# Expert pairs side by side, four experts gathered transposed, whole rows scattered, low residual halves in place

## The chip, the core and the metric

One NeuronCore of a Trainium2 chip runs the kernel. It has TensorE (matmuls, written to the eight banks of PSUM), VectorE, ScalarE, GpSimd, SyncE (here only issuing transfers) and 16 DMA engines. The metric is the time of one launch on the device in microseconds, the median of several runs; lower is better. All data are float32.
## The reference

A decoder layer on 512 tokens of width 1024: a mixing block (RG-LRU and pooling branches), then a mixture of experts, then a gated input embedding and a last norm. What matters here is the middle:

```python
u = rms_norm(h, norm_ffn_g[l])
# hierarchical_moe: best group of 4, best 2 of its 8 experts, for each token
expert_ids = g_idx[:, None] * EXPERTS_PER_GROUP + top_i      # 512 tokens x 2 choices, 32 experts
...
def expert_block(args):
    xblk, e = args
    h = jax.nn.silu(xblk @ w_gate_e[e]) * (xblk @ w_up_e[e])  # 1024 -> 512, twice
    return h @ w_down_e[e]                                    # 512 -> 1024
contrib = y[dest] * w_s[:, None]
return jax.ops.segment_sum(contrib, tok_s, num_segments=n)
...
h = h + moe_out
u = rms_norm(h, norm_ple_g[l])
h = h + sigmoid(u @ w_ple_gate[l]) * (p[l] @ w_ple[l])
```

## The kernel before

The program is one straight order of instructions for each engine, with semaphores between them. The first 355 us compute the mixing block. Matmuls there are made exact by splitting each operand in a high half and a low residual half (`split_high` on ScalarE, `split_low`), three fp32r products per matrix. The last two of its 15 weight blocks ("out") give the residual stream h1, whose rows are split too: `row_high` and `rows_split` (L364) write `rows_high` and `rows_low`. `transpose_h1` (L1256) and `logits` (L1268) make the router's logits, `route` the choices, `places` (L1279) and `find_places` the place of each token among the (at most 64 per round, C = 64) tokens of its expert.

Then comes a loop over the 32 experts, in rounds of 64 tokens for each; one round does in this case. All tokens sit in SBUF, and each expert's are picked by a matmul with a 0/1 matrix `pick` that VectorE makes (`make_pick`, L1017) for two experts at a time. `gather` multiplies `rows_high` and `rows_low` with it (stationary: pick, 128 columns for two experts; moving: 512 columns of the rows). ScalarE copies the gathered rows with their norm's scale (`gather_scale`, `copy_rows`, L764), TensorE transposes them (`transpose_x`, L1363), VectorE writes `xT` with the norm's gain (`copy_xT`, L1028). `gate_and_up` (L1375) multiplies one expert's 64 tokens with its gate and up matrices; the 64 tokens fill half of the array's columns, so two column halves of the weights run side by side. ScalarE takes the sigmoid, VectorE the two products, TensorE transposes the hidden rows (`transpose_hidden`, L1404), and `down` (L1390) of the expert before runs in between. VectorE scales the result by the gate (`scale_y`, L1108), and GpSimd scatters it to memory by row number, as half rows of 2 KB (`y_halves`), 128 of them for each expert. The row numbers and gates are gathered like the rows (`gather_info`).

Every matrix of an expert is a transfer of 2 MB (96 in all), issued by SyncE in the order in which TensorE wants them (`loads`) into a ring of nine slots (`LEAD`), `expert_slots`. Load n waits until load n - 9 has been read: a semaphore that TensorE raises after gate, up or down of that expert. The first loads wait for the end of the blocks before, the eighth and ninth for the logits and for the last `rows_split`, since their slots hold h1T and h1.

After the loop: the scatter's end, eight loads of the scattered rows, h1 restored from its halves, `add_choice` (L1159) for the sums, norm and transposes, and eight groups of 24 matmuls with the gate matrix `w_ple_gate`, which is split in high and low too (`gate_high`, `gate_low`, L357, in four steps).

All matmuls go through one helper, so they all stand at L1210 of the profile and are told apart by their tiles: `ring,junk` is gate or up, `ring,hT` down, `rounded,pick` the gather, `rstd,pick` the scale, `info,pick` row and gate, L1366 and L1407 the transposes of gathered and hidden rows. A name is the operand that moves first, then the stationary one.

## Time and profile before

| | us |
|---|---|
| median of 3 runs (lowest, highest) | 932.99 (931.66, 933.77) |
| the profiled execution's own time | 931.2 |
| its span, first to last instruction | 929.5 |
| TensorE busy, of the span | 896.1 (96%) |
| VectorE, ScalarE, GpSimd busy | 381.6, 243.5, 102.9 |
| DMA, mean over the span | 274 GB/s |
| granted clock of TensorE, mean | 0.991 |

All that follows comes from one profiled execution. Its times are microseconds from the first instruction, and differences between the execution's own time and the median belong to the run, not to the kernel. A busy TensorE is not one at its peak: matmuls overlap, and the time between the starts of two is what one costs.

### The profile page before, as it was taken

The numbers are of one execution on the slowest core, as the hardware profiler recorded it, in microseconds if no ns is written. First come the engines' busy times: TensorE is split into PE (matmuls) and PEld (weight loads), VectorE is DVE, ScalarE is ACT, GpSimd is POOL, SyncE is SP. The second block draws the span as 40 slices with busy tenths as digits, with TensorE's granted clock in tenths as the row PEclk, the third lists the DMA queues.
The fourth block names the chain that finished last, engine by engine and source line by source line (L and its number), as shares of the span: only waits on it lengthen the run. The fifth ranks groups of instructions, "written<-read, shape, count | busy, mean of one in ns | idle before, by whom it ended". The sixth has DMA issues, their size and how long they took to land.

```text
span 929.5 us, 12845 instructions
## 1 busy us (share of the span) xinstructions
PE 896.1 (96%) x5471; PEld 604.6 (65%) x5471; DVE 381.6 (41%) x617; ACT 243.5 (26%) x334; POOL 102.9 (11%) x80
## 2 busy tenths in 40 slices
PE   4999899999999997999999999999999999999996
PEld 3778677787888886656555555556555555554575
DVE  6699429953643427122212222122212222123875
ACT  6565337633332233100000000000000000001557
POOL 3338560000000000000000000000000000001000
PEclk9999999999999998999999999999999999999999
DMA  9222222212424446999999999999999999981702
GB/s 257 88 84 91 90 91 91 90 46 81 146 91 181 181 181 274 430 426 426 426 427 427 428 425 426 427 430 425 427 426 427 426 429 428 425 354 44 294 1 91
DMA packets 43297, 254.54 MB, mean 274 GB/s; under 512 B 8722, under 2 KB 9814, under 8 KB 30952
## 3 DMA queue, kind: packets, MB, share of 16 engines
q1 hardware_dynamic: 40392, 248.47, 65.7%
q0 software_dynamic: 2560, 4.20, 1.2%
q10 hardware_dynamic: 288, 1.05, 0.3%
q8 instruction: 43, 0.70, 0.3%
q14 instruction: 14, 0.11, 0.0%
HBM read 247.41 MB, written 10.49 MB: 277 GB/s over the span
## 4 chain that ended last, share of the span: by engine, by line
PE 86%; DVE 8%; ACT 3%; DMA 2%; issue 1%; DVEq 0%; SPq 0%; POOLq 0%; ACTq 0%
PE bank L1210 81%; PE bank L1366 2%; DVE ring L916 1%; PE bank L1407 1%; DVE ring L920 1%; DVE r L922 1%; ACT ring_rounded L345 1%; DVE ring_rounded L350 1%; DMA r<-in_x_dram 1%; DMA ring<-in_w_up_b_dram 1%; PE bank L1223 1%; DMA ring<-expert_rows 0%; DVE r L854 0%; PE bank L1264 0%; DVE ring L921 0%
## 5 line engine op out<-in xcount | busy, mean ns | idle before, releaser
L1210 PE MATMUL bank<-ring_rounded,ring_rounded 128*128 128x512 f32 x768 | 251.0, 392 | 1.7 <-ACT r L796 1.7
L1210 PE MATMUL bank<-r_rounded,ring_rounded 128*128 128x512 f32 x704 | 231.3, 399 | 4.7 <-DVE ring_rounded L350 2.8
L1210 PEld LDWEIGHTS bank<-ring_rounded,ring_rounded 128*128 128x128 f32 x768 | 144.6, 189 | 34.3 <-issue 2.4
L1210 PE MATMUL bank<-ring,junk 128*64 128x256 f32 x1408 | 166.1, 389 | 0.4 <-DVE junk L1030 0.4
L1210 PEld LDWEIGHTS bank<-r_rounded,ring_rounded 128*128 128x128 f32 x704 | 133.3, 190 | 36.5 <-DVE ring_rounded L350 3.6
L1210 PEld LDWEIGHTS bank<-ring,junk 128*64 128x64 f32 x1408 | 96.6, 134 | 61.4 <-issue 3.5
L1210 PE MATMUL bank<-ring,hT 128*64 128x512 f32 x512 | 119.8, 599 | 0.9 <-DVE hT L1115 0.9
L781 ACT ACTIVATE sig<-bank 128x256 f32<-128x256 f32 x32 | 12.3, 384 | 369.0 <-PE bank L1210 369.0
L591 POOL DMA_INDIRECT expert_rows<-r,row_i x32 | 31.7, 990 | 690.0 <-DVE r L1111 690.0
L1126 DVE TENSOR_TENSOR sig<-sig,bank 128x256 f32<-128x256 f32 x32 | 13.5, 421 | 218.3 <-ACT sig L781 218.3
L1210 PE MATMUL bank<-r,junk 128*64 128x256 f32 x640 | 76.4, 389 | 0.0
L350 DVE TENSOR_TENSOR ring_rounded<-ring,ring_rounded 128x2048 fp32r<-128x2048 f32 x19 | 43.5, 2288 | 55.1 <-ACT ring_rounded L345 55.1
L345 ACT ACTIVATE ring_rounded<-ring 128x2048 fp32r<-128x2048 f32 x28 | 53.6, 1913 | 43.8 <-DMA ring<-in_w_in_dram 19.2
L1210 PEld LDWEIGHTS bank<-ring,hT 128*64 128x64 f32 x512 | 32.9, 137 | 48.5 <-issue 46.6
L1210 PEld LDWEIGHTS bank<-r,junk 128*64 128x64 f32 x640 | 43.5, 134 | 28.1 <-issue 1.7
L1210 PE MATMUL bank<-r_rounded,pick 128*128 128x512 f32 x136 | 57.6, 425 | 0.0
L1210 PE MATMUL bank<-ring_rounded,pick 128*128 128x512 f32 x136 | 54.3, 401 | 0.0
L1111 DVE TENSOR_SCALAR r<-bank,gate_c 128x512 f32<-128x512 f32 x32 | 24.0, 751 | 70.3 <-PE bank L1210 70.3
L350 POOL TENSOR_TENSOR ring_rounded<-ring,ring_rounded 128x2048 fp32r<-128x2048 f32 x9 | 42.4, 4730 | 62.4 <-ACT ring_rounded L345 62.4
L1030 DVE TENSOR_TENSOR junk<-bank,gain_col 128x512 f32<-128x512 f32 x34 | 23.4, 691 | 52.6 <-PE bank L1366 52.6
L767 ACT ACTIVATE gain<-bank,row_scale 128x512 f32<-128x512 f32 x34 | 23.3, 687 | 73.4 <-PE bank L1210 73.4
L1210 PEld LDWEIGHTS bank<-r_rounded,pick 128*128 128x128 f32 x136 | 26.1, 192 | 11.2 <-issue 6.5
(195 smaller groups left out, 780.9 us busy)
## 6 DMA issues: line engine op xcount, KB each, us to landing
ring<-in_w_down_e_dram SPq DMA_DIRECT2D x32, 2048.0 KB, 14.5
ring<-in_w_gate_e_dram SPq DMA_DIRECT2D x22, 2048.0 KB, 11.8
ring<-in_w_up_e_dram SPq DMA_DIRECT2D x22, 2048.0 KB, 16.8
r<-in_w_up_e_dram SPq DMA_DIRECT2D x10, 2048.0 KB, 17.8
r<-in_w_gate_e_dram SPq DMA_DIRECT2D x10, 2048.0 KB
ring<-in_w_in_dram SPq DMA_DIRECT2D x18, 1024.0 KB, 7.3
r<-in_x_dram SPq DMA_DIRECT2D x8, 512.0 KB, 8.0
ring<-in_w_up_a_dram SPq DMA_DIRECT2D x4, 1024.0 KB, 6.3
```

What stands on the lines that cost most here:

```text
L345: nc.scalar.activation(high_half(n, h), whole_half(n, h), ACT.Copy).then_inc(high_ready, 1)
L350: api.tensor_tensor(low_half(n, h), whole_half(n, h), high_half(n, h), ALU.subtract).then_inc(low_ready[low_engine[n, h]], 1)
L591: nc.gpsimd.indirect_dma_start(out=y_halves, out_offset=bass.IndirectOffsetOnAxis(ap=row_i[:, e:e + 1], axis=0), in_=yrow[:, e % 4, :], in ...
L767: nc.scalar.activation(xrow[:, h * HALF:(h + 1) * HALF], bank[6 + h][:, :], ACT.Copy, scale=row_scale[:, 0:1]).then_inc(xrow_ready, 1)
L781: nc.scalar.activation(sig[:, :], bank[2 + e % 2][:, 0:FE // 2], ACT.Sigmoid).then_inc(sig_ready, 1)
L916: after(v.reciprocal(q, q))
L920: after(v.tensor_tensor(t, t, q, ALU.mult))
L1030: v.tensor_tensor(xT[:, 4 * h:4 * h + 4, :, :].rearrange("p k e c -> p k (e c)"), bank[6 + h][:, :].rearrange("p (k n) -> p k n", k=4), bc ...
L1111: v.tensor_scalar(yrow[:, e % 4, :], bank[5][:, :], gate_c[:, e:e + 1], None, ALU.mult).then_inc(y_stored, 1)
L1126: v.tensor_tensor(sig[:, :], sig[:, :], gate_up[:, 0:FE // 2], ALU.mult).then_inc(gated, 1)
L1210: return nc.tensor.matmul(*a, **k)
L1366: ins = nc.tensor.transpose(bank[6 + h][:, k * P:(k + 1) * P], xrow[:, h * HALF:(h + 1) * HALF].rearrange("p (q j) -> p j q", j=4)[:, k, : ...
```

## The change

- Experts run in pairs: `gate_or_up` and `down` stream the matrices of two experts side by side, 512 columns each, instead of two halves of one. The load order is changed to match, and a slot is given back when both experts of the pair have been read.
- Four experts (a "team") are gathered at once, and directly transposed: the rows are the stationary operand (one word of eight, `gather_k`), the pick matrix of 256 columns moves. Scale gather, row copy and `transpose_x` go; ScalarE copies PSUM to `xT` with the gain, and the scale of the norm is applied behind the gate and up products (`factor`). The first gather waits for all low halves before its second part.
- The scatter takes whole rows of 4 KB, both experts of a pair at once, 16 times instead of 32; two row buffers instead of four.
- `rows_low` is written in place of h1, and h1T moves to a smaller buffer, so that slots 1 and 2 of the ring (tiles 6 and 7) are free when the last two blocks start. The first load is issued one block sooner, two more by the next, and none waits for logits or residuals.
- The last two down matrices are loaded in halves. The gate matrix of the last stage gets its low half in place; all four steps of it are loaded ahead of the scattered rows and split before the first sum.

```diff
-    loads = [(0, 0), (1, 0)]
-    for e in range(1, NE):
-        loads += [(0, e), (1, e), (2, e - 1)]
-    loads += [(2, NE - 1)]
+    loads = [(which, e) for which in range(2) for e in range(2)]
+    for first in range(2, NE, 2):
+        loads += [(which, e) for which in range(2) for e in (first, first + 1)] + [(2, first - 2), (2, first - 1)]
+    loads += [(2, NE - 2), (2, NE - 1)]
     load_of = {matrix: n for n, matrix in enumerate(loads)}
...
-        yrow = r4[:, 0:4 * HALF].rearrange("p (b d) -> p b d", b=4)
-        xT = junk[:, :].rearrange("p (k e c) -> p k e c", k=KD, e=2)
-        xrow = gain[:, :]
+        yrow = r4[:, 0:2 * D].rearrange("p (b d) -> p b d", b=2)
+        def xT(k):
+            return (gain, junk)[k // 4][:, k % 4 * TEAM * C:(k % 4 + 1) * TEAM * C]
         rows_high = r2_r[:, :].rearrange("p (i d) -> p i d", i=TT)
-        rows_low = slot_r[6][:, :].rearrange("p (i d) -> p i d", i=TT)
-        pick = sb("pick", [P, 2, TT, 2, C], F32R)
-        hT = sb("hT", [P, KF, C])
-        sig = sb("sig", [P, FE // 2])
-        hid = sb("hid", [P, FE // 2])
+        rows_low = r1_r[:, :].rearrange("p (i d) -> p i d", i=TT)
+        pick = sb("pick", [P, TT, TEAM, C], F32R)
+        hT = sb("hT", [P, KF, 2 * C])
+        sig = sb("sig", [P, FE])
...
-        expert_slots = [ring[:, 0, :], ring[:, 3, :], ring[:, 4, :], ring[:, 1, :], ring[:, 2, :], ring[:, 5, :], r3[:, :],
-                        ring[:, 7, :], r1[:, :]]
+        expert_slots = [ring[:, 0, :], ring[:, 6, :], ring[:, 7, :], ring[:, 3, :], ring[:, 4, :], ring[:, 1, :], ring[:, 2, :],
+                        ring[:, 5, :], r3[:, :]]
...
             dve.wait_ge(rows_high_ready, i + 1)
+            dve.wait_ge(rows_psum, 2 * i + 2)
             nc.vector.tensor_tensor(rows_low[:, i, :], h1[:, i, :], rows_high[:, i, :], ALU.subtract).then_inc(rows_low_ready, 1)
...
+                    load_expert(0)
+            for n in range(1, LEAD):
+                sp.wait_ge(tile_done, 4 * (FIRST_OUT if n < 3 else FIRST_OUT + 1 if n < 5 else len(blocks)))
                 load_expert(n)
...
+                    sp.wait_ge((gate_psum, gate_up_psum, y_psum)[which], n0 + (e // 2 + 1))
+                for n in range(LEAD, 3 * NE - 2):
                     wait_expert_read(n - LEAD)
                     load_expert(n)
+                for n in (3 * NE - 2, 3 * NE - 1):
+                    wait_expert_read(n - LEAD)
+                    load_last_half(n, 0)
+                for n in (3 * NE - 2, 3 * NE - 1):
+                    load_last_half(n, 1)
...
-                    wait_expert_read(max(range(7, 3 * NE, LEAD)))
+                    wait_expert_read(max(range(6, 3 * NE, LEAD)))
                     sp.dma_start(wple, w_ple[0].rearrange("(k p) n -> p k n", p=P)).then_inc(ple_in, 16)
                     sp.dma_start(p_rows, p[0, 0].rearrange("(i p) n -> p i n", p=P)).then_inc(ple_in, 16)
-                    wait_expert_read(max(range(0, 3 * NE, LEAD)))
-                    load_gate(0)
-                    load_gate(1)
-            sp.wait_ge(row_free, rounds * NE + 4)
+                    wait_expert_read(max(range(8, 3 * NE, LEAD)))
+                    for step in range(4):
+                        load_gate(step)
+            sp.wait_ge(row_free, rounds * PAIRS + 2)
             for i in range(TT):
                 for k in range(2):
                     sp.dma_start(y_back(i, k), y_rows[k * S + i * P:k * S + (i + 1) * P, :]).then_inc(y_in[k][i], 16)
...
-                    pool.wait_ge(y_stored, n0 + (e + 2))
+                n0 = pool.snap(r * PAIRS)
+                for m in range(PAIRS):
+                    pool.wait_ge(y_stored, n0 * 2 + (2 * m + 4))
                     pool.sem_inc(rows_taken, 1)
                     nc.gpsimd.indirect_dma_start(
-                        out=y_halves, out_offset=bass.IndirectOffsetOnAxis(ap=row_i[:, e:e + 1], axis=0),
-                        in_=yrow[:, e % 4, :], in_offset=None, bounds_check=last_row,
-                        oob_is_err=False).then_inc(scattered[e % 4], 16)
-                    if e >= 2:
-                        release_row(n0, e - 2)
-                for e in (NE - 2, NE - 1):
-                    release_row(n0, e)
+                        out=y_rows, out_offset=bass.IndirectOffsetOnAxis(ap=row_i[:, m:m + 1], axis=0),
+                        in_=yrow[:, m % 2, :], in_offset=None, bounds_check=last_row,
...
+            def copy_xT(at, k, bank_):
+                act.wait_ge(xT_psum, at + (k // 2 + 1))
+                nc.scalar.activation(xT(k), bank_[:, k % 2 * TEAM * C:(k % 2 + 1) * TEAM * C], ACT.Copy,
+                                     scale=gain_col[:, k:k + 1]).then_inc(xT_ready, 1)
+            def sigmoid(n0, m):
+                act.wait_ge(factor_ready, n0 + (m + 1))
+                act.wait_ge(gate_psum, n0 + (m + 1))
+                if m >= 1:
+                    act.wait_ge(hT_psum, n0 + m)
+                nc.scalar.activation(sig[:, :], bank[2][:, :], ACT.Sigmoid, scale=factor[:, m, 1:2]).then_inc(sig_ready, 1)
+            for k in range(KD):
+                copy_xT(0, k, bank[4 + k // 2])
...
-            gate_high(0)
-            gate_high(1)
+            for step in range(4):
+                gate_high(step)
...
-                if i >= 2:
-                    gate_high(i)
...
-            def make_pick(pair, at=slice(0, TT)):
+            def make_pick(team, at=slice(0, TT)):
 
                 n = at.stop - at.start
-                v.tensor_tensor(pick[:, pair % 2, at, :, :], iota[:, :].unsqueeze(1).unsqueeze(1).to_broadcast([P, n, 2, C]),
-                                where.unsqueeze(3).to_broadcast([P, n, 2, C]), ALU.is_equal).then_inc(pick_ready, 1)
+                where = place[:, TEAM * team:TEAM * (team + 1), at].rearrange("p e i -> p i e")
+                v.tensor_tensor(pick[:, at, :, :], iota[:, :].unsqueeze(1).unsqueeze(1).to_broadcast([P, n, TEAM, C]),
+                                where.unsqueeze(3).to_broadcast([P, n, TEAM, C]), ALU.is_equal).then_inc(pick_ready, 1)
...
+            def take_info(n0, m):
+                dve.wait_ge(info_psum, n0 + (m // 2 * 2 + 2))
+                got = bank[5][:, m % 2 * 4:m % 2 * 4 + 3]
+                v.tensor_copy(factor[:, m, :], got[:, 1:3]).then_inc(factor_ready, 1)
+                v.tensor_scalar(row_i[:, m:m + 1], got[:, 0:1], row_base[:, 0:1], None, ALU.add).then_inc(row_ready, 1)
+            def make_hidden(n0, m):
+                dve.wait_ge(sig_ready, n0 + (m + 1))
+                v.scalar_tensor_tensor(out=sig[:, :], in0=bank[2][:, :], scalar=factor[:, m, 1:2], in1=sig[:, :], op0=ALU.mult,
+                                       op1=ALU.mult).then_inc(gated, 1)
+                dve.wait_ge(gated, n0 + (m + 1))
+                dve.wait_ge(gate_up_psum, n0 + (m + 1))
+                v.scalar_tensor_tensor(out=sig[:, :], in0=bank[3][:, :], scalar=factor[:, m, 1:2], in1=sig[:, :], op0=ALU.mult,
+                                       op1=ALU.mult).then_inc(hidden_ready, 1)
+            def scale_y(n0, m):
+                dve.wait_ge(y_psum, n0 + (m + 1))
+                dve.wait_ge(row_free, n0 + (m + 1))
+                for h in range(2):
+                    v.tensor_scalar(yrow[:, m % 2, h * HALF:(h + 1) * HALF], bank[h][:, :], factor[:, m, 0:1], None,
+                                    ALU.mult).then_inc(y_stored, 1)
+            def copy_hT(n0, m):
+                dve.wait_ge(hT_psum, n0 + (m + 1))
+                v.tensor_copy(hT[:, :, :], bank[4][:, :].rearrange("p (k c) -> p k c", k=KF)).then_inc(hT_ready, 1)
...
+                n0 = dve.snap(r * PAIRS)
+                for team in range(TEAMS):
+                    take_info(n0, 2 * team)
+                    take_info(n0, 2 * team + 1)
+                    make_pick((team + 1) % TEAMS)
+                    for m in (2 * team, 2 * team + 1):
+                        make_hidden(n0, m)
+                        if m >= 1:
+                            scale_y(n0, m - 1)
+                        copy_hT(n0, m)
+                scale_y(n0, PAIRS - 1)
...
-            gate_low(dve, v, 0)
-            gate_low(dve, v, 1)
+            for step in range(4):
+                gate_low(dve, v, step)
...
-                if i >= 2:
-                    gate_low(dve, v, i)
...
+            def gather_k(dst, k, i, **flags):
+                for part in (rows_high, rows_low):
+                    ins = mm(dst[:, k % 2 * TEAM * C:(k % 2 + 1) * TEAM * C],
+                             part[:, i, :].rearrange("p (q k) -> p k q", k=KD)[:, k, :],
+                             pick[:, i, :, :].rearrange("p e c -> p (e c)"), start=flags["start"] and part is rows_high,
+                             stop=flags["stop"] and part is rows_low)
+                return ins
+            def gather(at):
+                for k in range(KD):
+                    if k >= 4 and k % 2 == 0:
+                        pe.wait_ge(xT_ready, at + (k - 2))
+                    for i in range(TT):
+                        ins = gather_k(bank[6 + k // 2 % 2], k, i, start=(i == 0), stop=(i == TT - 1))
+                    if k % 2 == 1:
+                        ins.then_inc(xT_psum, 1)
...
+                    for e in (2 * m, 2 * m + 1):
+                        ins = mm(bank[5][e % 2 * C:(e % 2 + 1) * C, m % 2 * 4:m % 2 * 4 + 3], pick[:, i, e % TEAM, :].bitcast(F32),
+                                 info[:, e, i, :], start=(i == 0), stop=(i == TT - 1))
...
+            def gate_or_up(r, n0, m, which):
+                experts = (2 * m, 2 * m + 1)
+                for e in experts:
+                    wait_landed(r, load_of[which, e])
+                if which == 0 and m >= 1:
+                    pe.wait_ge(hidden_ready, n0 + m)
+                for k in range(KD):
+                    if which == 0 and m % 2 == 0:
+                        pe.wait_ge(xT_ready, n0 * 4 + (4 * m + k + 1))
+                    for e in experts:
+                        w = wslot(load_of[which, e], KD)
+                        ins = mm(bank[2 + which][e % 2 * C:(e % 2 + 1) * C, :], xT(k)[:, e % TEAM * C:(e % TEAM + 1) * C], w[:, k, :],
+                                 start=(k == 0), stop=(k == KD - 1))
+                ins.then_inc(gate_up_psum if which else gate_psum, 1)
+            def down(r, n0, m):
+                experts = (2 * m, 2 * m + 1)
+                pe.wait_ge(y_stored, n0 * 2 + (2 * m + 2))
+                pe.wait_ge(hT_ready, n0 + (m + 1))
+                if m == PAIRS - 1:
+                    pe.wait_ge(last_half, r * 32 + 32)
+                for k in range(KF):
+                    if k == (KF // 2 if m == PAIRS - 1 else 0):
+                        for e in experts:
+                            wait_landed(r, load_of[2, e])
                     for h in range(2):
-                        ins = mm(bank[5][h * C:(h + 1) * C, :], hT[:, k, :], w[:, k, h * HALF:(h + 1) * HALF],
-                                 start=(k == 0), stop=(k == KF - 1))
-                if ks[-1] == KF - 1:
-                    ins.then_inc(y_psum, 1)
-            def transpose_hidden(n0, e):
-                pe.wait_ge(hidden_ready, n0 + (e + 1))
-                for j in range(2):
-                    ins = nc.tensor.transpose(bank[4][:, j * P:(j + 1) * P], hid[:, j * P:(j + 1) * P], ident[:, :])
+                        for e in experts:
+                            ins = mm(bank[h][e % 2 * C:(e % 2 + 1) * C, :], hT[:, k, e % 2 * C:(e % 2 + 1) * C],
+                                     wslot(load_of[2, e], KF)[:, k, h * HALF:(h + 1) * HALF], start=(k == 0), stop=(k == KF - 1))
+                ins.then_inc(y_psum, 1)
+            def transpose_hidden(n0, m):
+                pe.wait_ge(hidden_ready, n0 + (m + 1))
+                if m >= 1:
+                    pe.wait_ge(hT_ready, n0 + m)
+                for k in range(KF):
+                    ins = nc.tensor.transpose(bank[4][:, k * P:(k + 1) * P], sig[:, :].rearrange("p (q k) -> p k q", k=KF)[:, k, :],
+                                              ident[:, :])
...
-            for h in range(2):
+            for k in range(KD):
                 for i in range(2):
-                    gather_from(0, h, i, rows_high, start=(i == 0), stop=False)
-                    gather_from(0, h, i, rows_low, start=False, stop=False)
+                    gather_k(bank[4 + k // 2], k, i, start=(i == 0 and k % 2 == 0), stop=False)
             places(1)
             pe.wait_ge(pick_ready, 2)
+            for k in range(KD):
+                for i in range(2, TT):
+                    ins = gather_k(bank[4 + k // 2], k, i, start=False, stop=(i == TT - 1 and k % 2 == 1))
+                if k % 2 == 1:
+                    ins.then_inc(xT_psum, 1)
...
+                n0 = pe.snap(r * PAIRS)
+                for team in range(TEAMS):
+                    gate_or_up(r, n0, 2 * team, 0)
+                    if team == 0:
+                        pe.wait_ge(info_made, 3)
+                    else:
+                        pe.wait_ge(row_ready, n0 + 2 * team)
+                    gather_info(2 * team)
+                    gather_info(2 * team + 1)
+                    gate_or_up(r, n0, 2 * team, 1)
+                    if team >= 1:
+                        down(r, n0, 2 * team - 1)
+                    transpose_hidden(n0, 2 * team)
+                    for which in range(2):
+                        gate_or_up(r, n0, 2 * team + 1, which)
+                    pe.wait_ge(pick_ready, r * TEAMS + (team + 3))
+                    gather(n0 * 4 + KD * (team + 1))
+                    down(r, n0, 2 * team)
+                    transpose_hidden(n0, 2 * team + 1)
+                down(r, n0, PAIRS - 1)
```

## Rows read from the trace of the kernel before

**Rows 1.** Windows, 461 to 551 us: each engine's busy time, clock, DMA share, GB/s.
```profile
461.00:551.00 90.00, 90.00 (x688) 51.32 (x686) 20.20 (x49) 6.43 (x12) 5.86 (x6) 1.00 1.01 427
```

**Rows 2.** Waits of SyncE's DMA queue, 365 to 860: us, times, longest.
```profile
SPq L456 <- PE bank L1210: 406.5, 87, 8.2
```

**Rows 3.** Timeline of SyncE: start, us, issue of a down matrix.
```profile
355.62 0.43 SPq L456 DMA_DIRECT2D ring<-in_w_down_e_dram  x1
...
805.20 4.47 SPq L456 DMA_DIRECT2D ring<-in_w_down_e_dram  x2
```

**Rows 4.** DMA issues of those moments: size, us from issue to landing.
```profile
ring<-in_w_down_e_dram SPq DMA_DIRECT2D x1, 2048.0 KB, 12.9
...
ring<-in_w_down_e_dram SPq DMA_DIRECT2D x1, 2048.0 KB, 18.6
```

**Rows 5.** Timeline of TensorE and VectorE, 581 to 596: start, busy us.
```profile
581.88 0.68 DVE L1021 TENSOR_TENSOR pick<-iota,place 128x512 fp32r<-128x512 f32 x1
...
588.53 1.05 PE L1210 MATMUL bank<-rstd,pick 128*128 128x1 f32 x8
...
589.45 0.48 PE L1210 MATMUL bank<-r_rounded,pick 128*128 128x512 f32 x1
...
589.76 0.39 PE L1210 MATMUL bank<-ring_rounded,pick 128*128 128x512 f32 x1
...
591.15 0.39 PE L1210 MATMUL bank<-ring_rounded,pick 128*128 128x512 f32 x1
...
591.47 0.63 PE L1210 MATMUL bank<-info,pick 128*64 128x2 f32 x16
...
591.96 3.63 PE L1210 MATMUL bank<-ring,hT 128*64 128x512 f32 x16
...
595.52 0.44 PE L1407 MATMUL bank<-ident,hid 128*128 128x128 f32 x2
```

**Rows 6.** Timeline of TensorE, 335 to 341: transposes of h1 and logits.
```profile
335.04 1.04 PE L1264 MATMUL bank<-ident,r 128*128 128x128 f32 x8
...
335.83 0.48 PE L1210 MATMUL bank<-ring_rounded,ring_rounded 128*128 128x512 f32 x1
...
338.67 1.87 PE L1210 MATMUL bank<-wrt,ring 128*128 128x36 f32 x16
...
340.37 0.48 PE L1210 MATMUL bank<-ring_rounded,ring_rounded 128*128 128x512 f32 x1
```

**Rows 7.** Timeline of TensorE and VectorE, the start of the loop.
```profile
362.20 0.40 PE L1210 MATMUL bank<-ring_rounded,pick 128*128 128x512 f32 x1
...
367.40 1.87 PE L1210 MATMUL bank<-rstd,pick 128*128 128x1 f32 x8 [1.03 <-DVE pick L1021]
...
375.05 1.12 PE L1210 MATMUL bank<-ring,junk 128*64 128x256 f32 x8 [0.42 <-DVE junk L1030]
...
366.92 0.42 DVE L1021 TENSOR_TENSOR pick<-iota,place 128x256 fp32r<-128x256 f32 x1
367.26 1.22 DVE L367 TENSOR_TENSOR ring_rounded<-r,r_rounded 128x1024 fp32r<-128x1024 f32 x1
```

**Rows 8.** Windows of 1 us, the start of the loop; clock third from last.
```profile
367.00:368.00 1.00, 0.60 (x3) 0.60 (x4) 1.00 (x2) 0.00 (x0) 0.00 (x0) 0.50 0.88 377
...
373.00:374.00 1.00, 0.70 (x5) 0.70 (x6) 0.00 (x0) 0.98 (x3) 0.00 (x0) 0.73 1.03 442
```

**Rows 9.** Timeline, 851 to 872: last down, low halves, first sums.
```profile
851.55 3.65 PE L1210 MATMUL bank<-ring,hT 128*64 128x512 f32 x16 [0.91 <-DVE hT L1115]
...
861.41 4.49 DVE L361 TENSOR_TENSOR ring_rounded<-ring,ring_rounded 128x2048 fp32r<-128x2048 f32 x2
...
865.82 3.62 DVE L1159 TENSOR_TENSOR r<-r,ring 128x1024 f32<-128x1024 f32 x3
...
871.54 1.06 PE L1223 MATMUL bank<-ident,r 128*128 128x128 f32 x8 [0.46 <-DVE r L854]
```

**Rows 10.** Window of 2 us in the last stage.
```profile
890.00:892.00 2.00, 1.18 (x10) 1.04 (x10) 0.91 (x1) 0.34 (x1) 0.00 (x0) 1.00 0.00 0
```

281 lines of the change are left out of this document (71 added, 210 removed).

## The prediction, on record before the changed kernel was seen

> **What bounds the kernel now.** I read four views in order. The windows come first: from 461 to 551 us TensorE is busy 90.00 of 90 us at full clock, and in the same window the DMA engines have a share of 1.01 at 427 GB/s [rows 1]. Two resources are full at once, so the question is which of them sets the end. The waits of the DMA queue answer half of it: SyncE, which issues the expert loads, waited 87 times and 406.5 us for TensorE to give a slot back [rows 2]. So TensorE paces the loop. The issue times and landings give the other half. Load 4 is issued at 355.62 and lands 12.9 us later, at 368.5. Load 94 is issued at 805.20 and lands 18.6 us later, at 823.8 [rows 3, 4]. That is 90 loads in 455.3 us, 5.06 us a load of 2.1 MB, and the time from issue to landing has grown: the transfers are slightly slower than TensorE and eat the ring's lead, without making it wait. A load alone cannot take under 2.1 MB / 427 GB/s = 4.91 us [rows 1]. The loop runs from 375.05 to 851.55 + 3.65 = 855.2 us [rows 7, 9], 30.0 us for two experts; the transfers want 6 x 5.06 = 30.4. Making TensorE faster therefore hands the loop to the DMA engines almost at once, and the loop's end then follows from when the loads start and how fast they run. The tail after 855.2 is 74.3 us of a span of 929.5.
>
> **TensorE's work for four experts, after.** Now: 2 x 30.0 = 60.0 us for four. After the change:
> - Gate, up and down are the same streams, 512 columns wide, two experts side by side. One down now is 16 instructions from 591.96 to 595.52, 3.56 us [rows 5]; a matrix of a pair is 32 of those, 7.12 less one handover of some 0.1: 7.05. Gate and up have the same count of columns as two downs each. Six pairs of matrices: 42.3 us.
> - The scale gather goes: 588.53 to the first gather at 589.45, 0.9 us a pair [rows 5], 1.8 for four. The transposes of the gathered rows go: 8 per pair in two groups. Eight transposes of h1 take 335.83 - 335.04 = 0.79 us [rows 6]; with 0.2 us of handover each group of four is 0.6, 2.4 for the four groups.
> - Gathers of row and gate: 0.49 each [rows 5], four now, two after: 0.98.
> - Transposes of the hidden rows: two groups of four at 0.6 and a little: 1.3, against four groups of two at 0.44 [rows 5].
> - The gather itself is what no row shows. Now it is 32 matmuls for four experts, 128 stationary columns and 512 moving: (591.15 - 589.76) / 6 = 0.232 us each [rows 5], 7.4 us. After it is 64 with 256 moving columns: the same columns, twice the weight loads. From below: half of 0.232 is 0.116, and matmuls of 36 columns with 128-wide stationary operands still take (340.37 - 338.67) / 16 = 0.106 us [rows 6], which is the weight load's own pace. From above: 0.232, as if nothing were won by the shorter stream. I take 0.13, the longer of stream (256 columns at 2.4 GHz, 0.107) and load (0.106) plus the 0.02 that the 512-column matmul has over its own 512 / 2.4 GHz = 0.213: 8.3 us. It is near the low end because loads are hidden in the 512-column rows: 0.106 of load and 0.213 of stream add to 0.32 there, and 0.232 is measured.
> - Sum: 42.3 + 8.3 + 1.0 + 1.3 = 52.9 us against 60.0.
>
> The Trainium skill speaks against this change at the gather. "TensorE: Matmul & The Clock Gate", Part 3, says that a weight load overlaps a running matmul only when the two use different row groups; these all use the full array. By that rule each gather matmul would cost load plus stream, 0.214 us, and 13.7 us for four experts. The 512-column rows already disagree with it (0.232, not 0.32), but no row shows a stream as short as its load, so the rule stays a rival. "SBUF — State Buffer", on 16-byte cachelines, says that reads which step past a line each time pay a penalty, and the new stationary operand takes every eighth word. The trace disagrees at this speed: the transposes of h1 have just such a stationary operand, one word of eight, and go at 0.79 / 8 = 0.099 us each [rows 6], no slower than the dense ones of the logits. I add nothing for it.
>
> **The transfers, after.** Twelve loads per four experts: 60.7 us against TensorE's 52.9, so the DMA engines bind. Loads 0 to 4 are now in before 355 us (three before), and loads 5 to 8 go at 355.3: four x 4.91 + 0.9 of latency end at 376. Load 9 needs the slot of expert 0's gate matrix, and that comes free, together with that of expert 1, only when the first pair's gate is done. The DMA engines idle until then; the head start of two loads is spent here.
>
> When is that? The second half of the first gather waits for the last low residual, now before its first matmul. VectorE's chain is 0.26 us longer by the selection, twice as wide (256 columns take 0.42 [rows 7], 512 take 0.68 [rows 5]), so the residual of 1.22 us that started at 367.26 [rows 7] ends at 368.8. TensorE's clock is then at half (0.50 at 367, 0.73 at 373 [rows 8]), so 32 matmuls x 0.213 = 6.8 us: gate starts at 375.6, against 375.05 [rows 7], because the scaled rows and their transposes are no longer behind the gather. The first half of the gather (32 x 0.13 = 4.2 us) lies in the wait before the second routing half. If the load does not hide at half clock this is 13.7 and the start 382.5.
>
> Gate of pair 0 ends at 375.6 + 7.05 = 382.7, load 9 starts. Loads 9 to 91 (up of the last pair) are 83 x 5.06 = 420.0 us, plus 0.9 latency and 2.5 by which a load in a queue lands after its turn (load 4 landed at 368.5; two loads from 355.25 are 355.25 + 0.9 + 9.8 = 366.0). That is 806.1. The nine slots suffice: the longest stretch with none given back is gather plus down, 8.3 + 7.05 = 15.4 us, three loads' worth. TensorE, with 7.8 us to spare per four experts, has caught up with the transfers after about three teams and then waits 2 to 3 us at a time. After load 91: up 7.05, the round's last gather (which nobody needs) 8.3, down 7.05, last down 7.05 = 29.5. Between the two downs VectorE must evict two banks (2 x 0.75) and copy the transposed hidden rows (0.7), and the last down waits for that copy: 2.3. The last loads land by 825 and bind nothing. End of the loop 806.1 + 31.8 = 837.9 instead of 855.2: **-17.3 us**.
>
> **The tail gives some back.** Before the first sum of expert rows (865.82) VectorE stood at the two low halves of the last gate matrix, 861.41 + 4.49 = 865.9 [rows 9]: it was exactly busy until the rows came. After, all four low halves lie ahead of the sums (+4.49), and the last expert rows take two evictions instead of one (+0.75, with the scatter behind them): +5.2 us. TensorE, done with the input embedding, waited 0.46 us there for the transposes at 871.54 [rows 9]; after, this idle becomes 5.7 us. The idle from 362.6 to 367.4 (with the few small matmuls of the routing in it) was some 4.8 us and left the clock at half until 373.7 [rows 7, 8], so I add half of the first 3.5 us of the last stage, 1.7. Back comes the wait at 890 to 892 (1.18 of 2.00 us busy [rows 10]), in which a low half stood in the way: -0.8. Tail: +5.2 + 1.7 - 0.8 = **+6.1**.
>
> Costed at nothing: whole rows in the scatter (same bytes, half the issues), GpSimd's work, ScalarE's eight copies per team (under the gather and the down behind it), the extra copy into the routing info (under the first gather). If the scatter's share of the DMA time (5.06 - 4.91 = 0.15 us a load) vanished, the loop would end 12 us sooner; half of it is all I allow.
>
> **Sum.** -17.3 + 6.1 = -11.2 us. The profiled execution took 931.2 us by its own time, span 929.5; this gives 920.0. The median shown is 932.99, 1.8 above it, so the forecast is **922 us**. A difference of under 0.2% (1.9 us) can't be told from none.
>
> **Rivals.**
> 1. Transfers bind, and they are quicker than now because whole rows scatter more cheaply, or the tail keeps its clock: 6 us of the scatter's 12 and the 1.7 of the clock: 914. For it: fewer, larger pieces; against it: the bytes are the same.
> 2. The weight load of the gather is not hidden (0.214 us). TensorE takes 44.6 + 13.7 = 58.3 us a team, 466 for eight; start at 382.5; with the 1.7 between the last downs the loop ends at 851. With the tail of 74.3 + 6.1 that is a span of 931, in the terms of the median **935**: no change. This is the page's rule above. Against it the 512-column rows; for it that nothing shorter has been seen.
> 3. Slower: a gather matmul costs what one of 512 columns costs, 0.232 or more, because the pace is that of the strided stationary read. Team 44.6 + 14.8 = 59.4, eight 475, start 383 (32 x 0.46 at half clock, from 368.8), loop end 860; with the tail **944**. It decides from a pitch of 0.21 up with that start (383 + 8 x (44.6 + 64 p) + 1.7 + 6.1 = 855.2), of 0.225 with the start at 375.6.
> 4. Each wait for a load drops the clock. A wait of 3 us is shorter than the idle that did it; and a slow team eats its own slack of 7.8 us, after which there is no wait. Only the last 30 us lie open: +3, 925. Inside the range of the forecast.
>
> **Numbers.** Forecast with rival 4: 0.62 (own range 916 to 930). Rival 1: 0.10. Rival 2: 0.14, spread from 929 to 938. Rival 3: 0.14. Faster by over 0.2%: 0.62 + 0.10 + a third of rival 2 = 0.77. Within 0.2%: 0.06, out of rival 2 (931 to 935). Slower: 0.17, rival 3 and the rest of rival 2. The range 913 to 937 leaves out rival 3 and a little at each end.
>
> **What would show it.** The gather: 64 starts per team, 0.13 us apart. SyncE's waits for TensorE shrink and TensorE shows idle time before gate, up and down, released by a DMA, from about 540 us on. The windows stay at 427 GB/s until about 825 us, with one dip at 376 to 383. The loop ends near 838. In the tail four low halves stand in a row before the first sum, and TensorE idles some 5 us before the first transposes. Wrong would make it: a pitch over 0.2; a start later than 377; a DMA rate under 427 in the loop; slots that starve the transfers.

## The result, and the profile after

The changed kernel takes **941.98 us** (median of 4 runs, 940.96 to 942.31) against 933.0 us (4 runs beside it, 931.66 to 933.77): ratio 1.0096, 95% interval 1.0078 to 1.0113. It is slower by 1%. The forecast was 922 in a range of 913 to 937, with 0.77 on faster; the price of rival 3, 944, is 2 us off. The profiled execution has a span of 940.6 us (929.5 before).

The first place to look is the one that no row of before could show: a team's gather. From the timeline of TensorE, changed kernel (start, busy us; a matmul's own bar is longer than the distance to the next):

```profile
410.04 15.68 PE L1209 MATMUL bank<-pick,r_rounded 128*128 128x256 f32 x64
425.65 0.64 PE L1209 MATMUL bank<-r,hT 128*64 128x512 f32 x1
```

64 gather matmuls in 425.65 - 410.04 = 15.61 us are **0.244 us each**, not 0.13: dearer than the 0.232 of a matmul with twice the columns [rows 5]. The chain of work that ended last shows the teams, one after another (start, us, what):

```profile
432.74 0.68 PE bank L1401 x4
433.42 21.68 PE bank L1209 x127
455.10 0.68 PE bank L1401 x4
455.79 36.57 PE bank L1209 x160
492.35 0.68 PE bank L1401 x4
```

It has matmuls and transposes alone. A team is 492.35 - 432.74 = 59.6 us; of that 15.6 is gather and 44.0 the rest, which the prediction had at 44.6. The windows and the waits of SyncE's queue, from 365 to 860 us, say the same from their side (columns as in [rows 1] and [rows 2]):

```profile
373.00:461.00 88.00, 87.06 (x451) 45.41 (x452) 13.46 (x28) 10.07 (x20) 2.15 (x2) 0.97 0.82 339
461.00:551.00 90.00, 90.00 (x432) 51.42 (x430) 10.04 (x17) 8.79 (x19) 1.93 (x2) 1.00 1.00 424
```

```profile
SPq L427 <- PE bank L1209: 394.6, 43, 21.9
```

TensorE is busy 90.00 of 90 us as before [rows 1], and the queue still waits for it, now in fewer and longer waits (43 and 394.6 us; 87 and 406.5 before [rows 2]). From 461 on the two kernels look alike; a lower rate stands earlier, 339 GB/s from 373 to 461 (427 in that stretch before). It comes from the start of the loop (timeline of TensorE, then of SyncE's queue):

```profile
361.05 7.92 PE L1209 MATMUL bank<-pick,r_rounded 128*128 128x256 f32 x32
368.82 0.19 PE L1209 MATMUL bank<-routed_bf,before 128*128 128x32 bf16 x1
...
371.79 7.94 PE L1209 MATMUL bank<-pick,r_rounded 128*128 128x256 f32 x32 [2.53 <-DVE r_rounded L373]
379.66 2.79 PE L1209 MATMUL bank<-ring,gain 128*64 128x512 f32 x12
```

```profile
356.90 0.62 SPq L427 DMA_DIRECT2D r<-in_w_down_e_dram  x1
386.79 0.33 SPq L427 DMA_DIRECT2D ring<-in_w_down_e_dram  x1
```

The first half gather takes 7.8 us, so the place sums wait for it and start only at 368.82; the second half takes 379.66 - 371.79 = 7.87 more. Gate starts at 379.66 (375.05 before [rows 7], forecast 375.6), load 9 goes at 386.79 (forecast 382.7). The windows of 2 us hold one more fact:

```profile
365.00:367.00 2.00, 2.00 (x10) 1.00 1.00 422
...
374.00:376.00 2.00, 2.00 (x10) 0.50 0.99 426
...
420.00:422.00 2.00, 2.00 (x10) 1.00 1.00 426
```

With 256 columns a stream would need at least 0.107 us at 2.4 GHz and 0.213 at 1.2, but the gather keeps its pace at a granted clock of 0.50 and of 1.00: 10 matmuls are to be seen in 2 us in each (all that have a part in the window, so more than start in it). The second half gather took 7.87 us with some 5.8 of them at 0.50, the first 7.8 with some 3 at 0.50, and a team's 15.6 are at 1.00 throughout. So neither a stream nor a sum of load and stream in TensorE's clock sets the pace; what does is for the experiments.

The last down (timeline of TensorE):

```profile
852.33 7.09 PE L1209 MATMUL bank<-ring,hT 128*64 128x512 f32 x32 [1.61 <-DVE hT L1127]
```

It ends at 859.4 (855.2 before), +4.2. From gate's start to there it is 479.8 us, against 480.2 before: the loop itself gains 0.4 us, and its start is 4.6 later. Then the tail (timeline of VectorE, then of TensorE; answers to [rows 9]):

```profile
865.92 4.49 DVE L366 TENSOR_TENSOR ring_rounded<-ring,ring_rounded 128x2048 fp32r<-128x2048 f32 x2
870.32 4.49 DVE L366 TENSOR_TENSOR r_rounded<-r,ring_rounded 128x2048 fp32r<-128x2048 f32 x2
874.72 2.48 DVE L1160 TENSOR_TENSOR r<-r,ring 128x1024 f32<-128x1024 f32 x2
```

```profile
880.45 1.94 PE L1222 MATMUL bank<-ident,r 128*128 128x128 f32 x8 [4.87 <-DVE r L866]
884.05 5.49 PE L1209 MATMUL bank<-ring_rounded,ring_rounded 128*128 128x512 f32 x12 [1.66 <-ACT ring L810]
```

The four low halves stand in a row before the first sum, TensorE waits 4.87 us (forecast 5.7, before 0.46), and comes back at half clock: 12 matmuls in 5.49 us. Tail: 940.6 - 859.4 = 81.2, against 74.3: +6.9 (forecast +6.1). The +4.2 at the loop's end and the tail's +6.9 are the 11.1 us between the two spans.

### The profile page after: what moved, and what is told of

Same layout as the page of the kernel before. It is cut to its first block, busy times and chain, and to the rows that moved or that the text cites. A ratio compares the mean times of both kernels' runs of the same rounds, so it can differ in the third digit from the quotient of the medians.

```text
span 940.6 us, 10137 instructions
## 1 busy us (share of the span) xinstructions
PE 904.1 (96%) x4223; PEld 592.0 (63%) x4223; DVE 341.2 (36%) x478; ACT 249.3 (27%) x356; POOL 87.5 (9%) x63
## 4 chain that ended last, share of the span: by engine, by line
PE 88%; DVE 8%; ACT 2%; DMA 1%; issue 1%; DVEq 0%; SPq 0%; POOLq 0%; ACTq 0%
PE bank L1209 85%; DVE ring L928 1%; DVE ring L932 1%; PE bank L1401 1%; PE bank L1222 1%; DVE r L934 1%; DMA r<-in_x_dram 1%; DMA ring<-expert_rows 0%; DVE r_rounded L366 0%; DVE ring_rounded L355 0%; PE bank L1263 0%; ACT ring_rounded L350 0%; DMA expert_rows<-r,row_i 0%; DVE ring L933 0%; ACT junk L623 0%
## 5 line engine op out<-in xcount | busy, mean ns | idle before, releaser
L1209 PEld LDWEIGHTS bank<-pick,r_rounded 128*128 128x128 f32 x576 | 139.8, 338 | 9.1 <-issue 9.1
L1209 PE MATMUL bank<-pick,r_rounded 128*128 128x256 f32 x576 | 141.7, 409 | 2.5 <-DVE r_rounded L373 2.5
L1209 PE MATMUL bank<-ring,gain 128*64 128x512 f32 x472 | 116.3, 596 | 0.0
L1209 PE MATMUL bank<-ring,junk 128*64 128x512 f32 x472 | 115.3, 592 | 0.0
L1122 DVE TENSOR_SCALAR r<-bank,factor 128x512 f32<-128x512 f32 x32 | 22.6, 746 | 224.6 <-PE bank L1209 224.6
L600 POOL DMA_INDIRECT expert_rows<-r,row_i x16 | 16.4, 1027 | 710.6 <-DVE r L1122 411.5
L1209 PEld LDWEIGHTS bank<-ring,junk 128*64 128x64 f32 x472 | 36.5, 137 | 73.1 <-issue 73.1
L1209 PEld LDWEIGHTS bank<-ring,gain 128*64 128x64 f32 x472 | 34.4, 137 | 61.3 <-issue 59.4
L1209 PE MATMUL bank<-r,hT 128*64 128x512 f32 x80 | 35.3, 594 | 0.0
L914 DVE SCALAR_TENSOR_TENSOR ring<-bank,prm,ring 128x511 f32<-128x511 f32 (+2 forms) x24 | 17.9, 747 | 36.3 <-ACT ring L659 35.7
```

The lines of the kernel that those rows point to most:

```text
L600: nc.gpsimd.indirect_dma_start(out=y_rows, out_offset=bass.IndirectOffsetOnAxis(ap=row_i[:, m:m + 1], axis=0), in_=yrow[:, m % 2, :], in_o ...
L914: ins = v.scalar_tensor_tensor(out=y[:, d:S], in0=z[:, 0:S - d], scalar=tap(3 - d, c), in1=y[:, d:S], op0=ALU.mult, op1=ALU.add)
L1122: v.tensor_scalar(yrow[:, m % 2, h * HALF:(h + 1) * HALF], bank[h][:, :], factor[:, m, 0:1], None, ALU.mult).then_inc(y_stored, 1)
L1209: return nc.tensor.matmul(*a, **k)
```

## The experiments

Each is compared with the kernel before, run beside it on the same chip (medians 931.9 to 932.5). Edits are to the changed kernel.

**1. A ladder of steps.** The two theories for the 0.244: the step between the words of the stationary operand (32 bytes), or the full-array weight load that isn't hidden behind a short stream (rival 2). The gather reads a step of 1, 2, 4 and 8 words for the four pairs of k (other features than the reference's), and so do the router's logits. One execution, 934.7 us.

```
- part[:, i, :].rearrange("p (q k) -> p k q", k=KD)[:, k, :]
+ part[:, i, 0:P * 2 ** (k // 2)].rearrange("p (q s) -> p s q", s=2 ** (k // 2))[:, 0, :]
```

> What it changes in the computation: in the changed kernel the stationary operand of each gather matmul is read with a step of 1, 2, 4 or 8 words for k = 0-1, 2-3, 4-5, 6-7 (always the same first words), and so is the stationary operand of the router's plain f32 logits, so the gathered and routed values are others. The profile after shows 0.244 us from start to start of the 256-column gather matmuls, at full clock (414.7) and at half clock (374) alike. Theory A (the strided read of the stationary fp32r operand sets the pace, at a clock that TensorE's gate doesn't touch): about 0.13 us at step 1, rising with the step to 0.244 at step 8. Theory B (a short stream can't hide its weight load: load plus stream plus handover, 0.106 + 0.107 + 0.02 to 0.03): 0.23 to 0.25 at every step, step 1 too. Theory C (the fp32r kind of weight load is slow in itself, 0.24, and 512-column streams hid it): the same at every step, like B, but independent of the clock. For the f32 logits, 0.106 us dense: A without a difference of kinds gives 0.2 or more at step 8; if fp32r alone suffers, it stays at 0.10 to 0.11.

The timeline of TensorE and windows of 1 us of its gather matmuls (busy, matmuls of which a part lies in it, clock, DMA share, GB/s), team 1:

```profile
415.14 11.70 PE L1209 MATMUL bank<-pick,r_rounded 128*128 128x256 f32 x64
```

```profile
418.10:419.10 1.00, 1.00 (x11) 1.00 1.00 426
419.10:420.10 1.00, 1.00 (x7) 1.00 1.03 442
420.10:421.10 1.00, 1.00 (x6) 1.00 0.96 410
```

There is one edge, halfway. Windows with the steps of 1 and 2 show 10 or 11 matmuls, those with 4 and 8 show 6, as everywhere in the changed kernel's gathers. 32 x 0.123 + 32 x 0.244 = 11.7 us, the whole bar. A step of 4 words costs what a step of 8 does, a step of 2 costs nothing. The logits' stationary operand is plain float32: 32 of them took 5.52 us where the changed kernel's dense ones take 3.7, so it is no matter of the rounded type. Nor does it need a long stream. The logits move 36 columns; of 16 of them, which took 339.65 to 342.37, the 8 at steps of 4 and 8 words cost (2.72 - 8 x 0.106) / 8 = 0.23 us each, an estimate with the dense ones at their pace of [rows 6].

**2. Dense stationary, and nothing else.** The gathers and no other reader take 128 adjacent words, so experts see features in another order than their weights.

```
+ part[:, i, k * P:(k + 1) * P]
```

> What it changes in the computation: the stationary operand of the gather is 128 neighbouring words of the row instead of every eighth, so the features come out in another order than the weights expect; all else is the changed kernel. Theory A (strided stationary read): gather pitch 0.13 us, TensorE 43.7 + 8.3 = 52 us a team instead of 59.3, the loop becomes bound by the transfers (60.7 us a team from 386 on would end up at 806 + 32 = 838 to 842), loop start 376 instead of 379.7, median 922 to 926. Theories B and C (no dependence on the step): pitch 0.24, median 942 as the changed kernel.

919.38 us (917.7 to 920.7), ratio 0.9866 (0.9847 to 0.9885). Timeline and windows:

```profile
405.11 7.94 PE L1209 MATMUL bank<-pick,r_rounded 128*128 128x256 f32 x64
412.98 0.64 PE L1209 MATMUL bank<-r,hT 128*64 128x512 f32 x1
```

```profile
461.00:551.00 90.00, 85.97 (x497) 38.38 (x495) 15.58 (x28) 7.94 (x17) 3.11 (x4) 1.00 1.01 428
```

64 in 7.87 us, **0.123** each, 0.01 from what was forecast. Rival 2, a load that isn't hidden, is gone with it: a full load of 0.106 [rows 6] and a stream of 0.107 fit into 0.123 only if they overlap. TensorE now stands idle here for 4.0 us of 90, and for 8.9, 9.1 and 10.9 in the next three windows, while the DMA engines stay at 426 to 428 GB/s: the transfers bind, and the last down ends at 835.7 (forecast 837.9). The tail keeps its 80.9. So the rest of the prediction's arithmetic held: it said 922, and the chip with a dense gather says 919.

Some of the waits also drop the clock, which the prediction had not expected of waits of 3 us. One of them (timeline of TensorE, then a window of 2 us with the columns of [rows 1]):

```profile
602.14 8.78 PE L1209 MATMUL bank<-ring,hT 128*64 128x512 f32 x32 [2.39 <-DMA ring<-in_w_down_e_dram]
```

```profile
603.00:605.00 2.00, 2.00 (x6) 0.49 (x4) 0.00 (x0) 0.00 (x0) 0.00 (x0) 0.50 0.95 397
```

The down takes 8.78 us, not 7.09. Behind a wait of 3.56 us at 622.68 the clock is at half again; behind one of 2.30 at 562.28 it stayed at 1.00, and what decides it no run here shows. The last down comes no later for it than forecast: TensorE has this time to spare behind the transfers.

**3. Dense by another layout of the weights.** The whole computation, with partition q of a gate or up tile holding rows k times 128 plus q; the gathers and the transposes of h1 read dense, and the 16 KB pieces of the gate and up loads become 2 KB. The down loads, a third of the bytes, keep theirs.

```
- w[0, e].rearrange("(p k) n -> p (k n)", p=P)
+ w[0, e].rearrange("(k p) n -> p k n", p=P)
```

> The same dense stationary operand with the features kept right: gate, up, router weights and the norm's gain are laid out with feature k*128+p at partition p, so gate and up arrive in pieces of 2 KB a row instead of 16 KB in one. The full computation. Theory A: as the dense gather, 922 to 926, if pieces of 2 KB go at the same 427 GB/s. A rival inside it: the smaller pieces cost bandwidth; then SyncE's transfers fall below 420 GB/s in the middle of the loop and the time follows them, 5% less bandwidth being some 16 us on two thirds of the bytes, 935 to 942. Theories B and C: 942.

946.81 us, ratio 1.0166 (1.0147 to 1.0185): slower than either.

```profile
461.00:551.00 90.00, 81.52 (x453) 36.05 (x453) 13.57 (x25) 7.11 (x15) 2.89 (x3) 0.96 1.04 401
```

The gather is at 0.123 and TensorE idle a tenth of the time, but the DMA engines, just as full (1.04), now move 401 GB/s. From gate's start to the end of the last down, at 864.3, the loop takes 6.5% longer than in experiment 2, and the pace of the transfers is 6% lower. The transposes of h1, which now read dense (timeline):

```profile
335.35 1.03 PE L1265 MATMUL bank<-ident,r 128*128 128x128 f32 x8
336.14 0.48 PE L1211 MATMUL bank<-ring_rounded,ring_rounded 128*128 128x512 f32 x1
```

**4. The tail alone.** Gate steps 2 and 3 go back behind the sums of tiles 2 and 3, on ScalarE and VectorE.

```
- for step in range(4):
-     gate_low(dve, v, step)
+ gate_low(dve, v, 0)
+ gate_low(dve, v, 1)
...
+ if i >= 2:
+     gate_low(dve, v, i)
```

> The changed kernel with steps 2 and 3 of the last gate matrix split where the kernel before had them (behind the transposes of row blocks 2 and 3) instead of ahead of the first sum. The tail after the last down is 81.2 us in the changed kernel and 74.3 before. Theory: the two low halves (4.5 us) in front of the first sum, and the half clock that the longer idle causes, are 6 of these 6.9 us: the first sum starts at 870.3 instead of 874.7, no half clock at 881 to 889, median 935.5 to 937.5. Rival: the first sum waits for the scattered rows anyway (they are issued at 865.3, 5.9 us after the last down against 5.05 before) and the gain is under 2 us, 940 or more.

935.9 us (935.2 to 936.8), ratio 1.0044 (1.0027 to 1.006), 6.1 us off the changed kernel. VectorE and TensorE:

```profile
869.92 3.62 DVE L1162 TENSOR_TENSOR r<-r,ring 128x1024 f32<-128x1024 f32 x3
```

```profile
875.64 1.06 PE L1226 MATMUL bank<-ident,r 128*128 128x128 f32 x8 [0.46 <-DVE r L868]
878.42 3.04 PE L1213 MATMUL bank<-ring_rounded,ring_rounded 128*128 128x512 f32 x12 [1.72 <-ACT ring L810]
```

The first sum comes 4.8 us earlier, the wait of 4.87 us is 0.46 again, and the 12 matmuls take 3.04 us instead of 5.49: the tail's loss was the two low halves, and the clock that TensorE lost over the wait. Tail 74.4. What is left of the slowdown, 4 us, stands at the start of the loop, and experiment 2 shows it to be the gather's.

**5. Permuted rows.** The whole computation with 16 KB loads: the residual sum writes its rows k-major, and everything up to the gathers reads them densely. Behind the loop, sums, norms and squares read natural order through a view. With the edit of experiment 4.

```
- res = h1[:, i, h * HALF:(h + 1) * HALF]
- v.tensor_tensor(res, res, bank[t % 4][:, :], ALU.add)
+ v.tensor_tensor(natural(h1p[:, i, :], 64 * h, 64 * h + 64), q_k(h1[:, i, h * HALF:(h + 1) * HALF]),
+                 q_k(bank[t % 4][:, :]), ALU.add)
...
- v.tensor_tensor(h1[:, i, :], h1[:, i, :], y_back(i, k), ALU.add)
+ v.tensor_tensor(natural(h1[:, i, :]), natural(h1[:, i, :]), q_k(y_back(i, k)), ALU.add)
```

> The whole computation, with 16 KB expert loads as in the changed kernel. The residual sum writes its rows with their features in the order k times 128 plus q, so that the h1 transposes and the gathers read 128 adjacent words; after the loop the sums read that order through a view. Gate steps 2 and 3 are split later, as in the tail run before. Theory A (the gather's price is the 32-byte step of its stationary): gathers at 0.123 us a matmul, teams at the pace of the DMA, 57 us each, as in the run with dense features: last down ends near 836 and the tail is 75, span 911, time 912 to 915, ratio 0.98 to the kernel before. Theory B (the strided reads that are now VectorE's and ScalarE's cost what TensorE's did): the strided sums behind the loop, some 25 of 0.6 to 1.1 us, double and the tail grows by 8 or more: 922 or over.

927.55 us (926.2 to 929.9), ratio 0.995 (0.9935 to 0.9966). Both theories have a part. The last down ends at 836.2, as said; the tail is 88.3 us, because VectorE's and ScalarE's work in it now reads and writes with a step of 128 words. The first sums (timeline of VectorE):

```profile
847.13 5.75 DVE L1170 TENSOR_TENSOR r<-r,ring 128x1024 f32<-128x1024 f32 x3
```

That is 1.92 us a sum, against 3.62 / 3 = 1.21 in experiment 4. Of the 13.9 us by which the tail is longer, 6.6 have gathered by the first product of the last stage (884.67, against 900.88 in experiment 4), by such sums and norms and by TensorE at half clock behind them; 7.2 come after it, where strided sums, squares and the last products take turns on the chain.

**6. The same with the loads late.** Loads 1 to 4 wait for the end of the output projection. One load is then ahead of it, where the change has five and the kernel before had three, so this undoes more than the change did.

```
- (FIRST_OUT if n < 3 else FIRST_OUT + 1 if n < 5 else len(blocks))
+ len(blocks)
```

> The permuted rows kernel, but expert loads 1 to 4 wait for the end of the output projection as loads 5 to 8 do, instead of going out in its first half: it undoes what the change does for the two ring slots and keeps the rest. If the early loads buy time only through bytes that are moved before the loop: four loads of 2.1 MB at 427 GB/s are 19.6 us of DMA work which then lies after 335 us, where the DMA is idle in part (377.5 to 386.8 in the changed kernel). Theory A (the loop of the permuted kernel is bound by the DMA from its start): 8 to 15 us slower than the permuted one. Theory B (the queue has slack before the loop, as in the changed kernel, whose DMA stood idle for 9 us at the loop's start): within 3 us of it.

939.98 us, 12.4 us slower than experiment 5. Four loads at 427 GB/s are 19.6 us, of which some 4, when the loads are late, fall into a stretch before load 9 in which experiment 5 moves nothing. Once the transfers bind, bytes moved ahead of the loop win most of their own time. What the two loads of the change alone are worth was not run. In the changed kernel the DMA engines stood idle for 9 us before load 9; whether the early loads brought anything there was not run either.

**7. Pieces of 4 KB.** Partition q of a gate or up tile has rows 256 g + 2 q and the next, so the stationary step is two words, which the ladder had as free. Rows stay in place, in natural order. With the edit of experiment 4.

```
- part[:, i, :].rearrange("p (q k) -> p k q", k=KD)[:, k, :]
+ part[:, i, k // 2 * 2 * P:(k // 2 + 1) * 2 * P].rearrange("p (q s) -> p s q", s=2)[:, k % 2, :]
...
+ w[0, e].rearrange("(g p s) n -> p g (s n)", p=P, s=2)
```

> The whole computation with rows in place in natural order, but expert gate and up matrices loaded so that partition q has rows 256 g + 2 q and 256 g + 2 q + 1: pieces of 4 KB, stationary step of two words (8 bytes). Gate steps 2 and 3 late. Theory A (a step of two words is free, and 4 KB pieces cost a part of what 2 KB pieces did, 400 against 427 GB/s): gathers at 0.123 us, GB/s 410 to 427, loop end 836 to 850, time 914 to 930. Theory B (any strided stationary costs double in the kernel, the ladder's second step being an accident of its mix): gathers at 0.244 us and loop end near 860: 936 or over.

**924.38 us** (923.5 to 926.2), ratio 0.9917 (0.9889 to 0.9944): the fastest whole kernel here, 17.6 us below the changed one.

```profile
405.17 7.95 PE L1218 MATMUL bank<-pick,r_rounded 128*128 128x256 f32 x64
413.05 0.64 PE L1218 MATMUL bank<-r,hT 128*64 128x512 f32 x1
```

```profile
461.00:551.00 90.00, 84.44 (x489) 38.61 (x490) 13.57 (x25) 7.93 (x17) 2.89 (x3) 1.00 1.02 416
```

64 matmuls in 7.88 us: a step of two words is free in a kernel that has no other. With pieces of 4 KB for gate and up the transfers run at 416 GB/s, 2.6% under the 427 with 16 KB, and the last down ends at 847.3 instead of 835.7. Tail 74.4.

**8. Places first.** In the changed kernel the place sums go ahead of the first half gather. I expected to learn whether the half gather, now 7.8 us, had better not stand before them.

```
+ places(1)
  pe.wait_ge(pick_ready, 1)
...
- places(1)
  pe.wait_ge(pick_ready, 2)
```

> The changed kernel with the place sums of tokens 256 to 511 issued ahead of the first half of team 0's gather, instead of behind it. Gather price as in the changed kernel, 0.244 us. Theory A (the first half gather, 7.9 us, held back the place sums and all behind them): places at 366, second pick and rows ready near 369.3, but both halves of the gather (15.7 us) then stand behind the place sums, so the loop starts at 382 to 383 against 379.7 and the time is 0 to 3 us longer than the changed kernel's, 942 to 945. Theory B (rows and picks are the later ones, the order of the two does not matter): loop start within 0.5 us of 379.7 and 942.

945.34 us (943.7 to 945.5), 3.4 us slower than the changed kernel (Theory A). From the timeline:

```profile
367.18 15.63 PE L1209 MATMUL bank<-pick,r_rounded 128*128 128x256 f32 x64
382.74 3.65 PE L1209 MATMUL bank<-ring,gain 128*64 128x512 f32 x16
```

Gate starts 3.1 us later. The half gather in the wait is still worth more than it delays.

**9. Permuted, and back behind the loop.** As 5, but the sum that puts the halves together again after the loop restores natural order, and only its four instructions are strided in the tail.

```
- v.tensor_tensor(h1[:, i, :], rows_high[:, i, :], rows_low[:, i, :], ALU.add)
+ v.tensor_tensor(q_k(h1n[:, i, :]), natural(rows_high[:, i, :]), natural(rows_low[:, i, :]), ALU.add)
```

> The whole computation: as the permuted rows kernel up to the loop's end, but the step that adds the two halves again after the loop (4 instructions of VectorE) reads them through the view and writes natural order to the ring slot that held the gated embeddings, which move to the high halves' place. So only 12 instructions are strided on VectorE (8 residual sums, 4 restoring sums) and none in the chain of the tail. Theory A (the permuted kernel's 88 us behind the last matmul of the loop, against 74.4 in the 4 KB kernel, come from the strided sums there, 1.96 against 1.23 us each): last down ends at 836, the restoring sums take 1.9 us each in place of 1.15 (3 us in all, of which the wait for the expert rows hides little), tail 75 to 78, span 911 to 914, time 914 to 917, ratio 0.98. Theory B (the longer tail of the permuted kernel is due to something else, such as the clock or ScalarE's strided squares alone): tail over 82, 921 or more.

927.92 us, ratio 0.9949 (0.9933 to 0.9965): no better than 5, so the expectation is missed, though the later sums are at 1.2 to 1.3 us again. The wait is new. GpSimd's timeline, and VectorE's beside it:

```profile
840.10 14.09 POOL L609 DMA_INDIRECT expert_rows<-r,row_i  x1 [8.41 <-DVE r L1134]
```

```profile
839.82 9.13 DVE L1164 TENSOR_TENSOR ring<-r_rounded,r_rounded 128x1024 f32<-128x1024 f32 x4
848.63 4.72 DVE L374 TENSOR_TENSOR ring_rounded<-ring,ring_rounded 128x2048 fp32r<-128x2048 f32 x2
859.68 3.80 DVE L1172 TENSOR_TENSOR ring<-ring 128x1024 f32<-128x1024 f32 x3 [6.33 <-DMA ring<-expert_rows]
```

The last scatter's issue on GpSimd takes 14.09 us, the one before it 0.96; it ends at 854.19, just after VectorE's uninterrupted work does, at 853.35. In the changed kernel, and in experiment 5, with the same four sums of VectorE in dense form, it took 1.77.

**10. Another ladder,** of 2, 3, 4 and 6 words, to see the edge (one execution, 926.2 us; other features than the reference's are gathered).

```
+ s=(2, 3, 4, 6)[k // 2]
```

> The changed kernel with another ladder of the gather's stationary step: 2, 3, 4 and 6 words for the pairs of k 0-1, 2-3, 4-5, 6-7 (it gathers other features than the reference, so the output is not the computation's). 16 matmuls of each. Theory A (what counts is how many of the words lie in one 16-byte piece of a partition): step 2 0.123 us, step 3 between (4 words in 3 pieces): 0.16 to 0.244, steps 4 and 6 0.244 alike; 64 matmuls in 11.7 to 13.7 us. Theory B (the price grows with the step, with no edge): step 3 0.18, step 4 0.24, step 6 0.36 or more.

```profile
406.95 12.40 PE L1209 MATMUL bank<-pick,r_rounded 128*128 128x256 f32 x64
```

```profile
408.90:409.90 1.00, 1.00 (x9) 1.00 0.92 393
409.90:410.90 1.00, 1.00 (x8) 1.00 1.08 459
...
411.90:412.90 1.00, 1.00 (x6) 1.00 1.00 426
```

6 a window from 411.9 to the end: steps 4 and 6 cost alike. The gather takes 419.29 - 406.95 = 12.34 us; less 32 x 0.244 and 16 x 0.123 that leaves 2.56 for step 3, 0.16 each. So the price goes with how many of the words share a piece of 16 bytes: two in each, free; one in each, double; four in three such pieces, between. Theory B, a price that grows with the step, is out.

**11. Restoring late.** As 9, but VectorE first splits the gate steps, and restores tile 0 when the expert rows are back and the others between the sums.

```
- for i in range(TT):
-     v.tensor_tensor(q_k(h1n[:, i, :]), natural(rows_high[:, i, :]), natural(rows_low[:, i, :]), ALU.add)
  gate_low(dve, v, 0)
  gate_low(dve, v, 1)
...
+ dve.wait_ge(y_in[0][0], 16)
+ restore(0)
```

> The kernel of the run before (permuted rows, natural order restored behind the loop), but the four restoring sums no longer run while the last scatter is issued: VectorE first splits gate steps 0 and 1, then restores tile 0 once the expert rows are back, and tiles 1 to 3 between the sums that follow. Theory A (the strided sums of VectorE held back GpSimd, whose last scatter took 14.09 us in that run against 1.77 in the others): the last scatter takes 1.8 us and lands after 3.5, the first sum comes some 12 us after the last matmul of the loop in place of 21.7, the restoring sums lie in the chain with 2.3 us for each of one or two, tail 78 to 81, span 914 to 918, time 917 to 920. Theory B (the scatter of that run was late for a reason of its own, such as the transfers beside it, or any work of VectorE holds it back): the scatter takes over 8 us again and the time stays at 925 or over.

928.23 us (927.0 to 929.5), ratio 0.995 (0.9937 to 0.9964). The mechanism that was expected is there, the time is missed:

```profile
841.24 0.96 POOL L609 DMA_INDIRECT expert_rows<-r,row_i  x1 [8.41 <-DVE r L1134]
```

```profile
847.82 2.38 DVE L1164 TENSOR_TENSOR ring<-r_rounded,r_rounded 128x1024 f32<-128x1024 f32 x1 [0.84 <-DMA ring<-expert_rows]
850.30 2.48 DVE L1173 TENSOR_TENSOR ring<-ring 128x1024 f32<-128x1024 f32 x2
```

The scatter is issued in 0.96 us and the first sum stands at 850.3, 11.3 us after the last down, not 21.8. But ScalarE's copies of the embeddings go where the high halves lay, and so now wait for each restoring sum; the first norm comes late, and TensorE falls to half clock. From the chain:

```profile
869.76 0.60 ACT r L820
870.41 5.34 PE bank L1230 x12
```

The tail is 927.7 - 839.0 = 88.7. One wait was traded for another of about its size.

## Why the prediction was wrong

**The step that failed** is "The gather itself": 0.13 us a matmul, with "I add nothing for it" on the stationary operand's step. It is 0.244 at that step, in the teams as in both halves of the first gather (experiment 1: the same matmul is 0.123 at a step of one or two words; experiment 2: with nothing but that changed, 919.4 us, and the transfers bind). 64 x 0.114 = 7.3 us a team, less 0.6 by which the rest was shorter, turned the forecast's 52.9 us of TensorE into 59.6 measured, and a bound that should have passed to the DMA engines never left TensorE.

**Why the row misled.** I had one row for a strided stationary operand, the transposes of h1 at 0.099 us [rows 6]. They have one: h1 is read with the same step of eight words. But in experiment 3, where h1 is read densely, the same eight transposes took 336.14 - 335.35 = 0.79 us, as before. Transposes don't feel the step, so they could not tell of a gather; I used a row of another kind of instruction as if it bore on this one. What sets them apart inside the chip no run shows. The other sign was there too: I called the bound "as if nothing were won by the shorter stream" and didn't ask what would make that so for every column count.

The Trainium skill had it: "SBUF — State Buffer", Specifications (TRN2), gives lines of 16 bytes with at least two hits in each for full bandwidth. The traces agree for the gathers: 0.123 us at steps of 1 and 2 words, some 0.16 at 3, and 0.244 at 4, 6 and 8; at 8 words it is the same at half clock as at full. They do not for the transposes. I had set the rule aside on the transposes' row.

**Rival 3** named the mechanism, and its sum, 944, came out 2 us high. That it came so near is in part luck. Team 59.4, measured 59.6. Start 383, measured 379.66: I had doubled the gather's price at half clock, and it does not change with the clock. From the start to the last down's end it had 477, measured 479.8, so the two misses nearly cancel. Its condition, a pitch from 0.21 up with that start or from 0.225 with 375.6, was met. It had a chance of 0.14 on the strength of that one row.

**Rival 2** (a load that isn't hidden, 0.214) is refuted: 0.123 is the pitch of a full-array load and a stream of nearly equal length. By the sentence that the prediction took from "TensorE: Matmul & The Clock Gate", Part 3, of the Trainium skill the two would go in turn; the trace disagrees (0.123 against 0.106 and 0.107 added up).

**Rival 4** stood on a premise that fails: waits of 3 us were held to be too short to drop the clock. In experiment 2 the clock falls to 0.50 behind waits of 2.39 and 3.56 us. Its other half, that a slow team eats its own slack, held: the last down ends where it was forecast, within 2.2 us.

**Right, by its own steps.** TensorE's work besides the gather: 44.6 forecast, 44.0 measured. The handover to the transfers once TensorE is faster, the windows at 427 GB/s, the dip at the start, the last down at 837.9: all in experiment 2 (835.7). The start with a short gather: 375.6; experiment 2 has 374.73, where the second half begins 0.45 us later than forecast and takes 5.5 us, not 6.8, as the clock comes back within it. No row gave the 0.9 us of latency in front of a load: in the changed kernel load 9, issued to idle engines with others close behind, lands 7.6 us after its issue, 2.7 more than its bytes take at 427 GB/s. The 2.3 us between the last two downs: from 850.08 to 852.33. The tail: +6.1, measured +6.9, and by the mechanism named (experiment 4 takes it back). Whole rows at nothing: the rate in the loop, 424 to 428 GB/s with TensorE bound and 426 to 428 with the DMA, shows no gain from them, and the tail lost its clock, so rival 1 found nothing in either.

**The start** was costed wrongly for the same reason: the half gather, "4.2 us in the wait", takes 7.8 and holds the place sums for 2.5 us (368.82; 366.28 in experiment 2), and the second half takes 7.9.

## What to carry to other kernels

A matmul whose stationary operand takes one float32 word out of every four or more costs double here (0.244 for 0.123 us at 256 moving columns); whether a stream of 512 columns would hide most of that was not run. Look at the step before counting columns, and arrange the data so that at least two words that are read lie side by side. Pay for that order where nothing waits: in the layout of the gate and up loads it cost DMA pace (416 GB/s with pieces of 4 KB, 401 with 2 KB, 427 with 16 KB), in VectorE's sums of the tail 0.7 us each.

An estimate for an operation with no row of its own should come from the same kind of instruction, and a rival that rests on a written rule deserves more than the chance that one unlike row leaves it. When a stage speeds up, ask which of the things that were free while another bound (load layout, early loads) begin to cost: four early loads were worth 12.4 us once the DMA was the bound.

## What the runs showed that I had not expected

- The gather's pace with a step of 32 bytes doesn't depend on TensorE's clock: 32 matmuls in 7.87 us with a granted clock of 0.50 for some 5.8 of them, 64 in 15.6 at 1.00.
- TensorE's clock fell to 0.50 behind waits of 2.39 and 3.56 us in the loop of experiment 2, and stayed at 1.00 behind one of 2.30.
- Transposes by TensorE take the same 0.79 us for eight with dense and with strided stationary operands.
- VectorE with a step of 128 words: 1.92 us for a sum of 1024 words a partition (one input and the output strided) against 1.21; 2.3 with both inputs strided, against 1.15.
- Strided sums of VectorE with two inputs from SBUF held back GpSimd's issue of an indirect DMA: 14.09 us with four of them beside it, 1.77 with four dense ones, 0.96 when they were moved away. The Trainium skill, "SBUF — State Buffer", Who interferes with whom, has such sums contend with GpSimd's reads and infers that descriptor writing is not touched; the traces show the issue held for the strided form (14.09 us) and little for the dense one (1.77, against 0.96). Why it lasted through the dense low halves behind them (848.63 to 853.35) stays open.
- Open as well: the exact law at a step of three words (0.16 us), and why transposes are exempt.
